# Finished down blocks copied out of PSUM by ScalarE and added by accumulating transfers, in a two-layer transformer trunk in float32

## The reference

```
h = rmsnorm(x, norm_mlp[l])                                   # 256 x 2048
x = x + jnp.square(jax.nn.relu(h @ w_up[l])) @ w_down[l]      # hidden width 8192
```

## Time and profile before

| | |
|---|---|
| median of 3 runs | 2675.41 us (2675.23 to 2683.97) |
| the profiled execution | 2675.23 us, span 2673.5 us |
| TensorE busy | 2657.3 us, 99% |
| VectorE busy | 2091.3 us, 78% |
| ScalarE busy | 1457.6 us, 55% |
| GpSimd busy | 127.7 us, 5% |
| granted TensorE clock, mean | 0.999 |
| HBM read and written | 535.15 MB and 38.04 MB, 214 GB/s over the span |

### The profile page before, as it was taken

One profiled execution on the slowest core, in us unless ns is written; L12 is line 12 of the kernel. 1 busy time (PEld: TensorE's weight loads), 2 busy tenths in 40 slices (PEclk: granted clock), 3 DMA queues, 4 the chain that ended last, 5 costly groups with the idle time before them and its releaser, 6 DMA issues.

```text
span 2673.5 us, 35035 instructions
## 1 busy us (share of the span) xinstructions
PE 2657.3 (99%) x13684; PEld 2237.3 (84%) x13684; DVE 2091.3 (78%) x2943; ACT 1457.6 (55%) x1881; POOL 127.7 (5%) x218
## 2 busy tenths in 40 slices
PE   9999999999999999999999999999999999999998
PEld 7788778888888888888888887788888888888887
DVE  5666568977799898997756755689678998989975
ACT  5545555545665655655545455555456556556554
POOL 0100000000100100100010000000001001000000
PEclk9999999999999999999999999999999999999999
DMA  7875545676665666756677655456677657566574
GB/s 251 240 239 169 181 158 184 228 242 235 231 235 197 228 224 201 248 206 227 234 231 231 215 178 177 157 201 226 225 257 237 224 198 251 202 223 234 192 241 152
DMA packets 179957, 575.52 MB, mean 215 GB/s; under 512 B 23016, under 2 KB 43028, under 8 KB 179664
## 3 DMA queue, kind: packets, MB, share of 16 engines
q1 hardware_dynamic: 166256, 536.94, 60.0%
q0 software_dynamic: 13008, 35.98, 4.7%
q10 hardware_dynamic: 528, 0.37, 0.1%
HBM read 535.15 MB, written 38.04 MB: 214 GB/s over the span
## 4 chain that ended last, share of the span: by engine, by line
PE 92%; DVE 5%; ACT 1%; DMA 1%; issue 1%; POOLq 0%; POOL 0%; ACTq 0%
PE acc L531 23%; PE acc L532 23%; PE acc L533 23%; PE acc L499 2%; PE acc L501 2%; PE acc L500 2%; PE att L499 2%; PE att L500 2%; PE att L501 2%; DVE w_lo L1340 1%; PE acc L548 1%; PE acc L549 1%; PE acc L547 1%; DVE w_lo L1319 1%; DMA raw<-in_w_main 1%; PE att_turn L499 1%
## 5 line engine op out<-in xcount | busy, mean ns | idle before, releaser
L1319 DVE TENSOR_TENSOR w_lo<-raw,w_hi 128x1024 fp32r<-128x1024 f32 (+1 forms) x766 | 920.8, 1212 | 373.6 <-ACT w_hi L890 371.7
L890 ACT ACTIVATE w_hi<-raw 128x1024 fp32r<-128x1024 f32 (+1 forms) x766 | 800.6, 1051 | 597.6 <-PE acc L533 453.6
L531 PE MATMUL acc<-w_hi,h_hl 128*128 128x512 f32 x1800 | 716.7, 398 | 2.7 <-DVE w_lo L1319 2.7
L533 PE MATMUL acc<-w_hi,h_hl 128*128 128x512 f32 x1800 | 710.0, 394 | 0.0
L532 PE MATMUL acc<-w_lo,h_hl 128*128 128x512 f32 x1800 | 709.6, 394 | 0.0
L531 PEld LDWEIGHTS acc<-w_hi,h_hl 128*128 128x128 f32 x1800 | 338.8, 188 | 81.7 <-issue 4.6
L533 PEld LDWEIGHTS acc<-w_hi,h_hl 128*128 128x128 f32 x1800 | 338.8, 188 | 79.3
L532 PEld LDWEIGHTS acc<-w_lo,h_hl 128*128 128x128 f32 x1800 | 339.3, 188 | 73.2
L1340 DVE TENSOR_TENSOR w_lo<-raw,w_hi 128x1792 fp32r<-128x1792 f32 x178 | 359.8, 2021 | 36.9 <-ACT w_hi L899 36.8
L531 PE MATMUL acc<-w_hi,o_hl 128*128 128x512 f32 x912 | 361.0, 396 | 0.0
L532 PE MATMUL acc<-w_lo,o_hl 128*128 128x512 f32 x912 | 359.9, 395 | 0.0
(11 more groups left out here) (325 smaller groups left out, 3629.0 us busy)
## 6 DMA issues: line engine op xcount, KB each, us to landing
raw<-in_w_main SPq DMA_DIRECT2D x928, 512.0 KB, 4.1
scratch<-spread SPq DMA_DIRECT2D x37, 512.0 KB, 3.0
moved<-scratch SPq DMA_DIRECT2D x148, 128.0 KB, 3.1
scratch<-spread POOLq DMA_DIRECT2D x30, 512.0 KB, 3.2
moved<-scratch POOLq DMA_DIRECT2D x120, 128.0 KB, 4.6
raw<-in_w_misc SPq DMA_DIRECT2D x16, 336.0 KB, 4.1
bias_b<-bias_rows POOLq DMA_DIRECT2D x32, 96.0 KB, 5.5
xs<-in_x SPq DMA_DIRECT2D x4, 512.0 KB, 7.1
```

The costliest lines, as they stand in the source:

```text
L531: nc.tensor.matmul(o, a_hi, hi[:, kk], start=(k == 0), stop=False)
L533: last = nc.tensor.matmul(o, a_lo, hi[:, kk], start=False, stop=fin)
L890: nc.scalar.activation(w_hi[s][:, 0:2 * width], raw[r][:, 0:2 * width], ACT.Copy).then_inc(hi_ready, 1)
L1319: nc.vector.tensor_tensor(w_lo[s][:, 0:2 * width], raw[r][:, 0:2 * width], w_hi[s][:, 0:2 * width].bitcast(F32), ALU.subtract).then_inc(lo ...
```

## The change

**Down blocks of groups 0 to 2.** `take_down` moves from VectorE to ScalarE, behind the split of the fourth chunk of the following unit (`then[3]`). ScalarE copies the side banks into `stage` and the main banks into `spread`, both free at that time. GpSimd then issues two accumulating transfers, `rest += stage` and `xs += spread` (`add_down`), which count up `down_added`. The first copy waits for the store of the last transposed block; each later one for the two transfers before it. TensorE waits for the copies (`down_out`) where it waited for VectorE. The next user of `stage` (`take_side` of the next group's second up block), of `spread` (`spread_u`) and of `rest` (`add_sides`) waits for `down_added`.

**Fourth up block.** Its transpose in groups 0 to 2 comes behind the split of the last chunk and the low part of the sums, instead of before both.

**Last group.** In the third up block's unit, the relu and square of the second block (`take_summed`) come before chunk 6 instead of 5, and its transpose one chunk later. In the fourth up block's unit, `take_side` and `take_summed` of the third block come one and two chunks later, its transpose two chunks later, the use of the second moved block one chunk later, and `add_sides(0)` right after the first split. These are the places that groups 1 and 2 have. The merged unit is as it was.

```diff
+            def add_down(l, g, n):
+                pool.wait_ge(down_out, downs_before(l, g, n) + 1)
+                pool.dma_start(rest[:, n], stage[:], accum_op=ALU.add).then_inc(down_added, 16)
+                pool.dma_start(xs[:, :, n * NB:(n + 1) * NB], down_main, accum_op=ALU.add).then_inc(down_added, 16)
...
-                for n in range(POOL_MOVES):
+                pass_on(l, E_U)
+                for g in range(GROUPS - 1):
+                    for n in range(NBLK):
+                        pass_on(l, E_U + g * NBLK + n + 1)
+                    for n in range(NBLK):
+                        add_down(l, g, n)
+                for n in range((GROUPS - 1) * NBLK + 1, POOL_MOVES):
                     pass_on(l, E_U + n)
...
# TensorE
-                    down(g * 64 + (C_MLP + 56), 1, adds(g, 1), 2, wide=WIDE[2])
-                    down(g * 64 + (C_MLP + 64), 0, adds(g, 2), 3, wide=WIDE[3])
-                    up(g * 64 + (C_MLP + 72), 1, adds(g, 3), 1, wide=WIDE_UP[1])
+                    down(g * 64 + (C_MLP + 56), 1, downs(g, 0), 2, wide=WIDE[2])
+                    down(g * 64 + (C_MLP + 64), 0, downs(g, 1), 3, wide=WIDE[3])
+                    up(g * 64 + (C_MLP + 72), 1, downs(g, 2), 1, wide=WIDE_UP[1])
...
# ScalarE
                 def take_side(g, n, end):
                     unit_done(end)
+                    if n == 1:
+                        act.wait_ge(down_added, downs_before(l, g, 0) * 32)
...
+                def take_down(g, n, end):
+                    unit_done(end)
+                    if n == 0:
+                        act.wait_ge(spread_ready, l * MOVES + E_U + (g + 1) * NBLK + 1)
+                        act.wait_ge(pool_stored, (l * POOL_MOVES + (g + 1) * NBLK + 1) * 16)
+                    else:
+                        act.wait_ge(down_added, downs_before(l, g, n) * 32)
+                    nc.scalar.activation(stage[:], wide_pair[1 - n % 2], ACT.Copy)
+                    nc.scalar.activation(down_main, acc_pair[1 - n % 2], ACT.Copy).then_inc(down_out, 1)
...
-                    for n in range(1, NBLK):
-                        run(g * 64 + (C_MLP + 40 + 8 * n), wide=WIDE[n], steps=steps_at(g, WIDE_AT[n]))
-                    run(g * 64 + (C_MLP + 72), (), {7: lambda: u_moved(g, 4)}, WIDE_UP[1], steps_at(g, AT_UP1))
+                    run(g * 64 + (C_MLP + 48), (), {3: lambda: take_down(g, 0, end + 48)}, WIDE[1], steps_at(g, WIDE_AT[1]))
+                    run(g * 64 + (C_MLP + 56), (), {3: lambda: take_down(g, 1, end + 56)}, WIDE[2], steps_at(g, WIDE_AT[2]))
+                    run(g * 64 + (C_MLP + 64), (), {3: lambda: take_down(g, 2, end + 64)}, WIDE[3], steps_at(g, WIDE_AT[3]))
+                    run(g * 64 + (C_MLP + 72), (), {3: lambda: take_down(g, 3, end + 72), 7: lambda: u_moved(g, 4)},
+                        WIDE_UP[1], steps_at(g, AT_UP1))
                 g, end = GROUPS - 1, base + 64 * (GROUPS - 1)
-                run(C_MLP + 64 * g + 16, {3: lambda: take_side(g, 1, end + 16), 5: lambda: take_summed(g, 1, sides_count(g, -1))},
+                run(C_MLP + 64 * g + 16, {3: lambda: take_side(g, 1, end + 16), 6: lambda: take_summed(g, 1, sides_count(g, -1))},
                     (), WIDE_UP[2], steps_at(g, AT_UP2))
-                run(C_MLP + 64 * g + 24, {3: lambda: take_side(g, 2, end + 24), 5: lambda: take_summed(g, 2, sides_count(g, 0))},
-                    {3: lambda: u_moved(g, 1)})
+                run(C_MLP + 64 * g + 24, {4: lambda: take_side(g, 2, end + 24), 7: lambda: take_summed(g, 2, sides_count(g, 0))},
+                    {4: lambda: u_moved(g, 1)})
...
# VectorE
-                    def second_and_third():
-                        u_moved(g, 2)
+                    def second_sums_and_spread():
+                        u_sums_lo(g, 2)
                         spread_u(g, 3)
-                    run(g * 64 + (C_MLP + 32), (), {6: second_and_third, 7: lambda: u_sums_lo(g, 2)},
+                    run(g * 64 + (C_MLP + 32), (), {6: lambda: u_moved(g, 2), 7: second_sums_and_spread},
...
-                run(C_MLP + 64 * g + 16, (), {3: lambda: add_up_sides(g, 1, NBLK - 1), 5: lambda: spread_u(g, 1)},
+                run(C_MLP + 64 * g + 16, (), {3: lambda: add_up_sides(g, 1, NBLK - 1), 6: lambda: spread_u(g, 1)},
                     WIDE_UP[2], steps_at(g, AT_UP2))
-                run(C_MLP + 64 * g + 24, {3: lambda: add_up_sides(g, 2, NBLK)},
-                    {3: lambda: u_moved(g, 1, False), 5: lambda: spread_u(g, 2), 6: lambda: add_sides(0)})
+                run(C_MLP + 64 * g + 24, {3: lambda: add_up_sides(g, 2, NBLK), 5: lambda: u_moved(g, 1, False)},
+                    {0: lambda: add_sides(0), 7: lambda: spread_u(g, 2)})
```

More of the change, by code:

```diff
@@ L54 @@
 ACT_UNITS = N_WIN + 2 * NBLK + GROUPS * NBLK
[L55 removed]
+DVE_UNITS = 2 * NBLK + NBLK + NBLK
 PIECES = NB // P
@@ L826, in before @@
                         acts(g, 1)()
-                        adds(g, 0)()
+                        if g:
+                            downs(g - 1, 3)()
+                        else:
+                            adds(0)()
                     return before
@@ L875, in _ @@
                     plain(two, c, c - 8, o_lhs, acc[1])
-                down(last + 48, 0, adds(GROUPS - 1, 1), 2)
+                down(last + 48, 0, adds(1), 2)
                 if l < DEPTH - 1:
-                    down(last + 56, 1, adds(GROUPS - 1, 2), 3)
+                    down(last + 56, 1, adds(2), 3)
                 else:
-                    last_unit(l * CHUNKS + last + 56, o_lhs, acc[1], adds(GROUPS - 1, 2))
+                    last_unit(l * CHUNKS + last + 56, o_lhs, acc[1], adds(2))
         @block.scalar
@@ L1812, in u_sums_lo @@
                         .then_inc(sums_took, 1)
-                def take_sides(n):
-                    nc.vector.tensor_tensor(rest[:, n], wide_pair[1 - n % 2], rest[:, n], ALU.add)
                 def add_sides(n):
+                    if n == 0:
+                        dve.wait_ge(down_added, downs_before(l + 1, 0, 0) * 32)
                     p2, p1, p5, p7 = (rest[:, n, t, i * HALF:(i + 1) * HALF] for t in range(TT) for i in range(2))
@@ L1836, in gain_block @@
                         chain.link(nc.vector.tensor_scalar(rest_sq[:], mean_sq[:], 1.0 / D, EPS, ALU.mult, ALU.add))
-                def take_down(g, n, end):
-                    dve.wait_ge(multiplied, end + SLOTS)
-                    take_sides(n)
-                    add_to_x(end, n, bank=1 - n % 2)
                 def steps_at(g, first):
```

31 lines of the change are left out of this document (20 added, 11 removed).

## The result

| | before | after |
|---|---|---|
| median | 2676.97 us (6 runs) | 2696.13 us (6 runs, 2694.78 to 2705.71) |
| the profiled execution | 2675.23 us, span 2673.5 us | 2697.09 us, span 2695.3 us |

The changed kernel is slower: ratio 1.0075, 95% interval 1.0061 to 1.0089, some 20 us. The prediction (2674.5 us, range 2670.5 to 2695) is wrong, in the middle and at the edge.

The account below looks back on a forecast made before the run. TensorE was taken as the bound. Last group's gaps gone (-2.4 us) plus a new layer 0 gap (+1.7) gave -0.7 from 2675.23, so 2674.5 us; everything else cost nothing. Range 2670.5 to 2695 us.

Parts of the forecast that it names:

- Part 3: Down blocks, GpSimd's accumulating transfers: two of 512 KB per block fit into the DMA engines' free time, at no cost.
- What bounds the kernel: Whole kernel: TensorE-bound to within some 4 us of what an edit here can reach; no outcome gains 0.5% (13 us).
- Part 1, the relief: 24 down blocks: two adds of 1.22 and 1.21 us leave VectorE, 58 us in all, worth nothing by itself.
- Part 2, the copies on ScalarE: Down blocks, behind the fourth chunk's split: two copies of 1.25 us each; low part by 783.2, lead 3.7 us, cost nothing.
- Landing: Accumulating pair: lands in about 4 to 7 us from below, 16.1 from above; 22 us allowed before TensorE notices.
- Price on the engines: DMA engines: a pair takes one to two times a copy's 3.7 us; 7.3 us by the skill's rule.
- Room: DMA engines, down blocks: busy 59%, so 8.7 of 21.1 us per block free; a pair fills it at 2.4 times a copy.
- Rival (b): Weight loads behind an accumulating pair: DMA engines become the bound; above 2707 us at three times a copy; chance 0.13.
- Part 4, the last group: Last group's new order: gains 2.4 us in all; late third down input costs 1.7 us in layer 0, none in layer 1.
- Priced at nothing: Fourth up block: early add of `rest`, about 3 us of VectorE, and transpose 1.8 us later; both at no cost.

## Why the prediction was wrong, point by point

**The step that failed** is the room in Part 3: that a pair fits as long as it takes less than the 8.7 us per block in which the engines are free on average. It measured 6.2 us and cost 20 us in all; 2 x 512 KB of plain copies, 3.0 us, cost nothing, so as issued here the room ended between 3.0 and 6.2 us.

**What bounds the kernel: right.** With the transfers nearly removed the change brings 0.1%. No outcome was a gain of 0.5%.

**Part 1, the relief: right in size and in worth.** 70.1 us measured in the stretch, 71 forecast.

**Part 2, the copies on ScalarE: right.** They take 1.0 us each (I took 1.25), and they cost nothing with tiny transfers. But the forecast of a lead of 3.7 us there looked at the copies alone. In the changed kernel the next split waits 1.2 us and VectorE's sums, which stand ahead of the low part, 2.9 us, both for weight loads. The low part ends at 785.79 instead of 783.2 and is 0.8 us ahead, less than the 1.5 us before.

**Part 3, the accumulating transfers: here it failed.** Three terms, one after the other:
- *Landing*: 7.2 and 10.6 us from issue, well below the 22 us allowed. ScalarE does not wait for them at the copies. Right in its verdict, though I wrote "a pair about 4 to 7 us" from below.
- *Price on the engines*: 6.2 us a pair, against 3.0 for plain copies of the same bytes at the same place, a factor of 2.1, and 1.7 times the 3.7 us that I had for a copy. This was inside my "one to two times". The Trainium skill ("Collectives: The Full Stack", "Why ReduceScatter is half of AllGather") says of ReduceScatter that its add reads two sources where a copy reads one. The estimate by that rule was 7.3 us, nearer than my low end, and the factor of 2.1 agrees with it.
- *Room*: "8.7 of 21.1 us per block are free", and the pair must hold 2.4 times a copy "to fill the room". **This step was wrong.** It divides an average. The free time lies where SyncE has no buffer to load into, and cannot be saved up: before the change its loads wait 2009 us in all for VectorE's low parts, and in group 0's down blocks they land 8 to 12 us ahead of TensorE, never more. Behind the fourth pair the weights get 142 GB/s where 188 are needed, and what is missed comes out of that lead. As issued here the room ended between 3.0 and 6.2 us a pair, not at 8.7; with the two transfers apart 6.2 us nearly fit. My sum had no term for how close the two follow each other.

**Rival (b) had the place and not the size.** I let it decide from 2.4 times a copy and gave 33 us at three times. It decided at 1.7 times. I had also said that a DMA share over nine tenths would show it; over the down blocks it came at 0.86 (0.93 in the first of the four units), and at 0.88 it was nearly gone (0.96 in the first). And the gaps are not "behind the fourth chunks of the down blocks", where I would have looked, but most of them in the up blocks behind them, where VectorE has hardly any idle time.

**Part 4, the last group: mechanism right, size short.** Alone it costs 1.4 us in layer 0 (forecast 1.7) with a hand-over of 14.45 us (1241.39 to 1255.84; I took 14.1). In layer 1 I forecast no gap, with a hand-over of 12.9 us; it took 14.3 us (2568.13 to 2582.47), and two gaps of 0.85 and 0.9 us came. The mis-sized term is layer 1's hand-over, taken from a single row of that layer. In the changed kernel the same place in layer 0 is worse: the transposed block of 1250.02 is used at

```profile
1266.52 1.06 ACT L981 ACTIVATE o_hl<-moved 128x1024 fp32r<-128x1024 f32 x1 [7.01 <-DMA moved<-scratch]
```

16.5 us later, the long end of my range, and TensorE stands for 2.84 us. That it is long here is seen; whether the accumulating transfers, long over by then, have a part in it was not tested.

**Priced at nothing and confirmed:** the early `add_sides`, and the fourth block's later transpose; both are in the kernels that measure 0.9989 to 0.9996.

**The chances.** The forecast had 0.60 and rival (b) 0.13. The evidence for (b) stood in my own working: price unknown by a factor of two, a share of 0.59 before, and a lead of 1.5 us on one engine. A load that takes a queue from 36 to 61 MB next to a stream that may never be late should have had more.

## What to carry to other kernels

Free time on a shared resource is room only for what fits between the deadlines of the stream beside it. Take the stream's need (here 188 GB/s), take what it gets while the guest runs, and compare the shortfall with the lead that the stream needs at its tightest place (here low parts 2 to 3 us ahead at the third up block); the average share tells neither. If work must go there, issue it in parts that leave the stream time to catch up, and look for the damage not where the transfer runs but at the next stretch where the engine behind has no idle time.

And test a place by its complement, but look in the trace whether what is left runs as it ran: removing the fourth pair removed the loss, and that pair alone caused none, but alone its two transfers started 7 to 9 us apart instead of 0.6.

## What the runs showed of the hardware

- An accumulating transfer within SBUF held the DMA engines 2.1 times as long as a copy of the same size (6.2 and 3.0 us per 1 MB pair). Landing rose less: 7.2 and 10.6 us against 6.4 and 8.0 us.
- Accumulating transfers of 256 KB issued soon after one another were each held up at the issue, for 3.5 to 6.2 us in the first block, by something that the profile doesn't name. Whole ones showed it too, 46 us in eight issues of the changed kernel, and so did plain copies, 37 us in six issues, so it doesn't come from the accumulation. It decides which transfers of a kernel go back to back.
- The granted clock fell behind a short stop. In the changed kernel TensorE stood still for 2.84 us ahead of 1272.36, and from 1273.01 on seven distances between matmuls were 0.42 to 0.43 us instead of 0.23:

```profile
1272.00:1277.00 5.00, 4.64 (x13) 3.72 (x14) 4.86 (x8) 1.62 (x2) 0.00 (x0) 0.66 0.65 198
```

  The clock of this stretch is 0.66 of full speed, a mean of the two levels 1.2 and 2.4 GHz; this cost 1.6 us beside the gap itself. In the changed kernel without the last group's order the same came behind a stop of 1.85 us (at 1049.46, clock 0.58 from 1049 to 1053); behind one of 1.86 us in the changed kernel (at 2212.12) it did not. What decides between these two the runs don't tell.
